# Handing over between stages by token tile, with a layer's modulation split between its attention and the feed-forward before it

## The chip, the cores and the metric

One core of a Trainium2 chip runs the whole kernel. The metric is the device time of one execution in microseconds (us). TensorE multiplies; VectorE, ScalarE and GpSimd work on data beside it; SyncE issues the large DMA transfers. In the profile PE is TensorE, PEld its weight loads, DVE VectorE, ACT ScalarE, POOL GpSimd and SP SyncE.

## The reference

A stack of four layers in fp32 with 256 tokens and a width of 1024, followed by one larger "latent" layer. Each of the four layers is an attention (layer 0 and 3 stick-breaking, 1 MoBA, 2 sliding window) and a gated feed-forward of width 2816; what goes into each is a normalised x, shifted and scaled by a modulation that is computed from a vector c.

```
for i in range(DEPTH):
    mod = silu(c) @ ada_w[i] + ada_b[i]                 # 1024 x 6144
    sh1, sc1, g1, sh2, sc2, g2 = split(mod, 6)
    h = rms_norm(x, norm_gain[i, 0]) * (1 + sc1) + sh1
    x = x + g1 * attention[i](h)                        # w_in, heads, w_out
    h = rms_norm(x, norm_gain[i, 1]) * (1 + sc2) + sh2
    x = x + g2 * ((silu(h @ w_gate[i]) * (h @ w_up[i])) @ w_down[i])
...
mod, mod_c = silu(c) @ w_ada + b_ada, silu(c_ctx) @ w_ada + b_ada   # latent layer: also for a context
...
```

## The kernel before

**Matrix multiplication.** A fp32 product is made of three TensorE passes (L1878 to L1880): each weight and each input is split into a high and a low part, and high x high, low x high and high x low are added up in PSUM. Weights come in units of 4 k-tiles (128 rows each) by 512 columns, 1 MB, into a ring of four buffers `raw`. ScalarE casts a unit into w_hi (L856), VectorE subtracts for w_lo (L1311), both double buffered, so the conversion of unit u + 2 waits until unit u is multiplied. SyncE issues the loads in the order of one list, `loads`, and a buffer is free again when VectorE is through with it.

**Modulation.** The 1024 x 6144 matrix of a layer comes through the same ring as 24 further units ("ada"). TensorE is not used for their product: VectorE multiplies each unit by 128 entries of c and adds it to an accumulator `acc` of 128 x 2048 (`modulation_units`, L1327, 2.35 us). Eight units make a block, three blocks a layer, and `acc` is double buffered over blocks; GpSimd sets a new one to zero and loads its bias (`start_sums`). Then TensorE sums over the 128 partitions (`modulation`): as rows (pieces r1 and r2, the gates g1 and g2; L1916) or as columns (pieces c0, c1 and c2, the shifts and scales; L1924), and ScalarE copies the result out (L867, L873). Block 0 holds c0, block 1 holds r1 and c1, block 2 holds c2 and r2. For the latent layer the first eight units are accumulated a second time, into `acc_c`, for the context.

**What sets the order.** Each engine's program is written out. The tables ADA_MIX, ADA_UP and ADA_DOWN say behind which step of an attention, of the up half or of the down half of a feed-forward an ada unit is loaded and accumulated; SUMS says where the sums stand. Steps of an attention are numbered n; two make a panel of 512 columns, and SLOTS places the steps of the softmax between them. Before, attention 0 takes 16 units (its own blocks 1 and 2), attentions 1 and 2 take 8 (the next layer's block 0), attention 3 none, and the feed-forwards 24, 16, 16 and 24.

**Between two stages.** The last product is in two halves of 512 columns. VectorE multiplies each by its gate and adds it to x_res (`residual`, L1385 and L1389; half 1 can start only at the end of the last unit). ScalarE takes the squares (L897), VectorE and ScalarE the root for both token tiles of 128 together, VectorE scales the rows to n_st (L1372), TensorE transposes them (L1896), ScalarE applies gain, scale and shift and casts, VectorE takes the low part (L1346), and the next unit can be multiplied. In a feed-forward the same path from gate x up (act_st, L1538) through a transpose (L2113) leads into the down half, whose 22 k-tiles per half of the columns are taken as five units of 4 and a last one of 2.

## Time and profile before

| | us |
|---|---|
| median of 3 runs | 2442.58 |
| lowest and highest run | 2432.83, 2444.14 |
| the profiled execution | 2443.3 |
| its span in the trace | 2441.5 |
| TensorE busy in it | 1987.2 (81%) |
| VectorE busy in it | 1402.3 (57%) |
| ScalarE busy in it | 956.5 (39%) |
| accumulations (L1327), 120 in all | 281.9 |

A busy TensorE is not one at its full clock: the granted clock (PEclk) is shown beside it as a share of 2.4 GHz. The stages that are spoken of below: attention 0 from 52 to 210 us, feed-forward 0 to 431, attention 1 to 644, feed-forward 1 to 866, attention 2 to 1038, feed-forward 2 to 1259, attention 3 to 1409, feed-forward 3 to 1648, then the latent layer to the end.

### The profile page before, as it was taken

To read this page: it belongs to the slowest core of one execution; us is meant where nothing else is said; L and a number is where in the kernel's file an instruction comes from. 1 tells how busy PE (TensorE), PEld (TensorE's weight loads), DVE (VectorE), ACT (ScalarE), POOL (GpSimd) and SP (SyncE) were. 2 spreads that over 40 slices of the span, in tenths; PEclk is the share of its full clock that TensorE was granted. 3 is DMA by queue.
4 is the path that set the end of the run, shared out by engine and by line. 5 is a ranking of instruction groups with operands and counts; after the bars stand their busy time and mean duration, and the time that the engine had idled before them with its cause. 6 is when DMAs were issued, how large, how long until landed. Compare 5 with 4: busy or idle time off the path is not lost.

```text
span 2441.5 us, 34110 instructions
## 1 busy us (share of the span) xinstructions
PE 1987.2 (81%) x14354; PEld 1608.0 (66%) x14354; DVE 1402.3 (57%) x1415; ACT 956.5 (39%) x1353; POOL 108.6 (4%) x135
## 2 busy tenths in 40 slices
PE   3887999765699984679989869996878878767998
PEld 2665787554578763468767657875666677765787
DVE  5774768655466564366644578574335663445554
ACT  3454443333444342344445534334223411224543
POOL 1000000101000011000000000001000112000000
PEclk9998999887799987689999979897879898978999
DMA  7653879542288662167753347683113100023553
GB/s 279 251 212 113 276 251 331 192 174 69 69 269 279 208 222 75 52 203 259 246 172 121 114 161 248 216 317 137 54 52 104 35 4 3 17 86 109 173 189 104
DMA packets 215117, 393.42 MB, mean 161 GB/s; under 512 B 11306, under 2 KB 130102, under 8 KB 199606
## 3 DMA queue, kind: packets, MB, share of 16 engines
q1 hardware_dynamic: 214453, 391.12, 46.9%
q8 instruction: 114, 1.87, 0.3%
q14 instruction: 38, 0.30, 0.0%
q0 software_dynamic: 512, 0.13, 0.0%
HBM read 390.17 MB, written 1.05 MB: 160 GB/s over the span
## 4 chain that ended last, share of the span: by engine, by line
PE 62%; DVE 18%; ACT 11%; issue 6%; DMA 2%; POOL 1%; DVEq 0%; SPq 0%; ACTq 0%
PE G L1878 15%; PE G L1879 15%; PE G L1880 15%; DVE w_lo L1311 6%; ACT w_hi L856 4%; DVE acc L1327 4%; PE A L1924 2%; PE A L2336 2%; PE A L1916 1%; PE A L1896 1%; ACT z_sb L966 1%; PE A L2113 1%; PE G L2350 1%; PE A L1984 1%; POOL e_sb L741 1%
## 5 line engine op out<-in xcount | busy, mean ns | idle before, releaser
L1311 DVE TENSOR_TENSOR w_lo<-raw,w_hi 128x2048 fp32r<-128x2048 f32 (+1 forms) x256 | 569.8, 2226 | 515.6 <-ACT w_hi L856 510.8
L856 ACT CAST w_hi<-raw 128x2048 fp32r<-128x2048 f32 (+1 forms) x256 | 475.2, 1856 | 688.9 <-PE G L1880 590.7
L1878 PE MATMUL G<-w_hi,h_hi 128*128 128x512 f32 (+1 forms) x1376 | 559.8, 407 | 90.0 <-DVE w_lo L1311 47.9
L1879 PE MATMUL G<-w_lo,h_hi 128*128 128x512 f32 (+1 forms) x1376 | 546.9, 397 | 0.0
L1880 PE MATMUL G<-w_hi,h_lo 128*128 128x512 f32 (+1 forms) x1376 | 545.4, 396 | 0.0
L1878 PEld LDWEIGHTS G<-w_hi,h_hi 128*128 128x128 f32 x1376 | 270.0, 196 | 152.9 <-issue 73.3
L1880 PEld LDWEIGHTS G<-w_hi,h_lo 128*128 128x128 f32 x1376 | 269.4, 196 | 57.1
L1879 PEld LDWEIGHTS G<-w_lo,h_hi 128*128 128x128 f32 x1376 | 270.1, 196 | 52.5 <-issue 0.5
L1878 PE MATMUL G<-w_hi,act_hi 128*128 128x512 f32 (+2 forms) x704 | 282.7, 401 | 20.2 <-DVE act_lo L1346 10.5
L1327 DVE SCALAR_TENSOR_TENSOR acc<-raw,c_col,acc 128x2048 f32<-128x2048 f32 x120 | 281.9, 2349 | 25.1 <-DVE w_lo L1311 12.6
L1879 PE MATMUL G<-w_lo,act_hi 128*128 128x512 f32 (+2 forms) x704 | 278.0, 395 | 0.0
L1880 PE MATMUL G<-w_hi,act_lo 128*128 128x512 f32 (+2 forms) x704 | 277.3, 394 | 0.0
L1878 PEld LDWEIGHTS G<-w_hi,act_hi 128*128 128x128 f32 x704 | 138.3, 196 | 52.2 <-DVE act_lo L1346 12.5
L1880 PEld LDWEIGHTS G<-w_hi,act_lo 128*128 128x128 f32 x704 | 138.0, 196 | 28.3
L1879 PEld LDWEIGHTS G<-w_lo,act_hi 128*128 128x128 f32 x704 | 138.6, 197 | 27.1 <-issue 0.5
L1346 DVE TENSOR_TENSOR act_lo<-full,act_hi 128x512 fp32r<-128x512 f32 (+1 forms) x86 | 57.7, 679 | 112.8 <-ACT act_hi L882 104.9
L1896 PE MATMUL A<-consts,n_st 128*128 128x128 f32 x176 | 34.9, 381 | 58.7 <-DVE n_st L1372 54.3
L753 POOL MEMSET acc<- 128x2048 f32 x15 | 27.1, 1808 | 1167.6 <-PE A L1924 996.6
L1924 PE MATMUL A<-consts,acc 128*128 128x1 f32 x320 | 45.6, 274 | 39.7 <-DVE acc L1327 35.3
L1896 PEld LDWEIGHTS A<-consts,n_st 128*128 128x128 f32 x176 | 31.4, 204 | 68.3 <-DVE n_st L1372 56.3
L1924 PEld LDWEIGHTS A<-consts,acc 128*128 128x128 f32 x320 | 46.1, 228 | 43.4 <-DVE acc L1327 36.3
L2043 PE MATMUL A<-consts,z_sb 128*128 128x128 f32 x32 | 8.9, 435 | 71.4 <-DVE z_sb L1491 71.4
(350 smaller groups left out, 2052.9 us busy)
## 6 DMA issues: line engine op xcount, KB each, us to landing
raw<-in_ada_w SPq DMA_DIRECT2D x96, 1024.0 KB, 5.1
raw<-in_ffn_w_gate SPq DMA_DIRECT2D x88, 512.0 KB, 3.9
raw<-in_ffn_w_up SPq DMA_DIRECT2D x88, 512.0 KB, 5.0
raw<-in_ffn_w_down SPq DMA_DIRECT2D x40, 1024.0 KB, 5.1
raw<-in_w_mlp SPq DMA_DIRECT2D x32, 1024.0 KB, 5.6
raw<-in_w_ada SPq DMA_DIRECT2D x24, 1024.0 KB, 5.0
raw<-in_w_in SPq DMA_DIRECT2D x18, 1024.0 KB, 5.0
raw<-in_sb_w_in SPq DMA_DIRECT2D x32, 512.0 KB, 4.7
```

The source lines that it names most:

```text
L741: ins = nc.gpsimd.tensor_tensor(dst[:, :, :, a:a + 32], src[:, :, :, b:b + 32], for_heads(rope_t[:, 1, t, tabs, a:a + 32], heads // (tabs. ...
L753: nc.gpsimd.memset(acc[:, b % 2], 0.0).then_inc(acc_zero, 1)
L856: nc.scalar.copy(w_hi[:, u % 2, 0:len(kts), 0:n], raw[:, slot].rearrange("p (k n) -> p k n", k=UNIT_K)[:, 0:len(kts), 0:n])\
L1311: nc.vector.tensor_tensor(w_lo[:, u % 2, 0:len(kts), 0:n], raw[:, slot].rearrange("p (k n) -> p k n", k=UNIT_K)[:, 0:len(kts), 0:n], w_hi[ ...
L1327: nc.vector.scalar_tensor_tensor(out=acc[:, b % 2], in0=raw[:, slot], scalar=c_col[:, c:c + 1], in1=acc[:, b % 2], op0=ALU.mult, op1=ALU.a ...
L1346: nc.vector.tensor_tensor(dst_lo, full[:, f % 2, 0:SEQ * dst_lo.shape[1]].rearrange("p (a n) -> p a n", n=SEQ), dst_hi.bitcast(F32), ALU.s ...
L1878: nc.tensor.matmul(banks[t][:, 0:n], x_hi[:, kt, ts], w_hi[:, u % 2, i, 0:n], start=st, stop=False)
L1879: nc.tensor.matmul(banks[t][:, 0:n], x_hi[:, kt, ts], w_lo[:, u % 2, i, 0:n], start=False, stop=False)
L1880: ins = nc.tensor.matmul(banks[t][:, 0:n], x_lo[:, kt, ts], w_hi[:, u % 2, i, 0:n], start=False, stop=en)
L1896: ins = nc.tensor.transpose(A[q][:, i * SEQ + t * P:i * SEQ + t * P + P], n_st[:, t, (2 * q + i) * P:(2 * q + i + 1) * P], ident)
L1924: ins = nc.tensor.matmul(banks[0][:, dst:dst + 1], x[:, c * P:c * P + P], ones[:, 0:1], start=True, stop=True)
L2336: ins = nc.tensor.matmul(A[c][half_of(1 - ch), cols_of(h)], LT[half_of(ch), c, cols_of(h)], X[half_of(ch), c, cols_of(h)], start=True, sto ...
```

## The change

It does two things.

**Hand-over by token tile.** After the last unit's products for token tile 0 TensorE gives a signal of its own (`tile_done`), and the last half's residual is taken tile by tile (`last_residual`, inside `norm`). Squares, root, scaling and the transposes of k-tiles 0 to 3 go tile by tile as well, and so do the splits behind them (128 x 4 x 128 instead of 128 x 512); k-tiles 4 to 7 go as before. One Newton step for the root takes two VectorE operations on one tile instead of four on both. A unit now waits for the split of its own tile (`ready_at`). The conversion of unit 1 stands between the tile splits and the others. The down half starts with the unit of 2 k-tiles (`down_kts`) instead of ending with it.

**Modulation.** Every attention takes 16 ada units, its own layer's blocks 1 and 2, spread evenly over its panels' steps; feed-forwards 0 to 2 take 8 (the next layer's block 0, three units of weights apart), feed-forward 3 takes 24 for the latent layer, spread from its second unit on. The sums r1 and c12 (c1 and c2 in one piece of 16 columns) stand behind the second step of the output projection of every attention, r2 behind up panel 1, c0 behind the down half's unit 8; in feed-forward 3 c0 stands behind up panel 7 and r1 behind down 2, and c12 and r2 behind the latent layer's first panel. The load of consts_2 goes out six loads later.

```diff
         for l in range(DEPTH):
-            first = KT if l in (1, 2) else 0
-            for i in range(first, ADA_U):
-                p = max(0, i - first - 2)
...
+            slots = 2 * len(qkv_panels(KINDS[l])) + 1
+            for i in range(2 * KT):
+                ADA_MIX[l].setdefault(i * slots // (2 * KT), []).append((l, KT + i))
+            n, first = (KT, 4) if l < DEPTH - 1 else (ADA_U, 2)
+            for i in range(n):
+                unit = first + i * (2 * FF // 256 + 6 - first) // n
+                if unit < 2 * (FF // 256):
+                    ADA_UP[l].setdefault(unit // 2, []).append((l + 1, i))
                 else:
...
+        SUMS = {(l, ("up", 1)): (l, "r2") for l in range(DEPTH)}
+        SUMS |= {(l, ("down", 8)): (l + 1, "c0") for l in range(DEPTH - 1)}
+        SUMS |= {(DEPTH - 1, ("up", 7)): (LAT, "c0"), (DEPTH - 1, ("down", 2)): (LAT, "r1")}
...
+        def down_kts(h):
+            return range(max(0, 4 * h - 2), 4 * h + 2)
...
@@ ScalarE, norm @@
-                rsqrt(NT)
-                for piece in sums or []:
-                    modulation(l, piece)
+                for t in range(NT):
+                    if x_end is not None and t == 0:
+                        k.tails += 1
+                        act.wait_ge(x_half, k.tails)
+                    elif x_end is not None:
+                        act.wait_ge(x_ready, x_end)
+                    square_of(t, 1, x).then_inc(ss_ready, 1)
+                    rsqrt(slice(t, t + 1))
...
@@ VectorE, norm @@
+                if last is not None:
+                    last_residual(0, *last)
+                mean_square(0)
+                if last is not None:
+                    last_residual(1, *last)
+                scale_rows(0)
+                mean_square(1)
+                scale_rows(1)
+                for t in range(NT):
+                    split(lo[:, 0:KT // 2, t * P:t * P + P], hi[:, 0:KT // 2, t * P:t * P + P])
                 between()
-                for q in range(KT // 2):
+                for q in range(KT // 4, KT // 2):
                     split(lo[:, 2 * q:2 * q + 2], hi[:, 2 * q:2 * q + 2])
...
@@ VectorE, mean_square and scale_rows @@
+                    nc.vector.scalar_tensor_tensor(out=rms_v[:, t:t + 1], in0=ssq[:, t, 1:2], scalar=1.0 / D, in1=ssum[:, t:t + 1],
+                    link(nc.vector.scalar_tensor_tensor(out=z, in0=y, scalar=y, in1=v, op0=ALU.mult, op1=ALU.mult))
+                    link(nc.vector.scalar_tensor_tensor(out=z, in0=z, scalar=-3.0, in1=y, op0=ALU.add, op1=ALU.mult))
+                    nc.vector.tensor_scalar(n_st[:, t], x[:, t], z, -0.5, ALU.mult, ALU.mult).then_inc(n_ready, 1)
...
@@ TensorE, unit @@
+                    if ready is not None:
+                        pe.wait_ge(split_lo, ready[t])
...
+                    if tiles and t == 0:
+                        ins.then_inc(tile_done, 1)
...
@@ TensorE, attention @@
-                        if l == 0 and n == 2 * len(panels) + 1:
-                            modulation(0, "r1")
-                            modulation(0, "c1")
+                        if n == 2 * len(panels) + 1:
+                            modulation(l, "r1")
+                            modulation(l, "c12")
...
-                if l == 0:
-                    modulation(0, "c2")
-                    modulation(0, "r2")
                 norm_transposes()
```

Where the order moves. VectorE, in the gap behind attention 1 (layer 1): n_st<-G,gates and x_res<-x_res,n_st are a residual, gsc the gain and scale, ssum to rms_y the root, h_lo the low parts for the feed-forward. Before:

```order
L1389 TENSOR_TENSOR x_res<-x_res,n_st 128x512 x2
L1385 TENSOR_TENSOR n_st<-G,gates 128x512 x2
L1389 TENSOR_TENSOR x_res<-x_res,n_st 128x512 x2
L1369 TENSOR_TENSOR ssum<-ssq 128x2
L1353 TENSOR_SCALAR rms_v<-ssum 128x2
L1355 TENSOR_TENSOR rms_t<-rms_y 128x2
L1356 TENSOR_TENSOR rms_t<-rms_t,rms_v 128x2
L1357 TENSOR_SCALAR rms_t<-rms_t 128x2
L1358 TENSOR_TENSOR rms_y<-rms_y,rms_t 128x2
L1372 TENSOR_SCALAR n_st<-x_res,rms_y 128x1024 x2
L1362 SCALAR_TENSOR_TENSOR gsc<-mod,cols 128x8
L1311 TENSOR_TENSOR w_lo<-raw,w_hi 128x2048
```

and now:

```order
L1377 SCALAR_TENSOR_TENSOR gsc<-mod,cols 128x8
L1385 TENSOR_SCALAR ssum<-ssq 128x2
L1426 TENSOR_TENSOR n_st<-G,gates 128x512
L1432 TENSOR_TENSOR x_res<-x_res,n_st 128x512
L1389 SCALAR_TENSOR_TENSOR rms_v<-ssq,ssum 128x1
L1426 TENSOR_TENSOR n_st<-G,gates 128x512
L1432 TENSOR_TENSOR x_res<-x_res,n_st 128x512
L1397 SCALAR_TENSOR_TENSOR rms_t<-rms_y,rms_v 128x1
L1398 SCALAR_TENSOR_TENSOR rms_t<-rms_t,rms_y 128x1
L1399 TENSOR_SCALAR n_st<-x_res,rms_t 128x1024
L1389 SCALAR_TENSOR_TENSOR rms_v<-ssq,ssum 128x1
L1397 SCALAR_TENSOR_TENSOR rms_t<-rms_y,rms_v 128x1
```

The residual of the second half is cut into tiles, and each tile's root and scaling follow one another; what is behind, the conversion w_lo, now stands after the first two splits.

VectorE, from the gap behind feed-forward 1 into attention 2 (ss_81 is the first operation of its query and key norm). Before:

```order
L1311 TENSOR_TENSOR w_lo<-raw,w_hi 128x4x256
L1346 TENSOR_TENSOR h_lo<-full,h_hi 128x512 x4
L1327 SCALAR_TENSOR_TENSOR acc<-raw,c_col,acc 128x2048
L1311 TENSOR_TENSOR w_lo<-raw,w_hi 128x2048
L1327 SCALAR_TENSOR_TENSOR acc<-raw,c_col,acc 128x2048
L1311 TENSOR_TENSOR w_lo<-raw,w_hi 128x2048
L1327 SCALAR_TENSOR_TENSOR acc<-raw,c_col,acc 128x2048
L1422 TENSOR_REDUCE ss_81<-e_sb 128x4
```

and now:

```order
L1361 TENSOR_TENSOR h_lo<-full,h_hi 128x4x128 x2
L1325 TENSOR_TENSOR w_lo<-raw,w_hi 128x4x256
L1361 TENSOR_TENSOR h_lo<-full,h_hi 128x512 x2
L1341 SCALAR_TENSOR_TENSOR acc<-raw,c_col,acc 128x2048 x3
L1325 TENSOR_TENSOR w_lo<-raw,w_hi 128x2048
L1341 SCALAR_TENSOR_TENSOR acc<-raw,c_col,acc 128x2048 x2
L1325 TENSOR_TENSOR w_lo<-raw,w_hi 128x2048
L1341 SCALAR_TENSOR_TENSOR acc<-raw,c_col,acc 128x2048 x2
L1478 TENSOR_REDUCE ss_81<-e_sb 128x4
```

Seven accumulations instead of three stand ahead of that norm.

TensorE, at the end of attention 1 (A<-aT,v_st are the last weighted values, G<-w_hi,act_hi begins another unit of the output projection). Before:

```order
L1984 MATMUL A<-aT,v_st 64x256
L1985 MATMUL A<-aT,v_st 64x128
L1984 MATMUL A<-aT,v_st 64x256
L1985 MATMUL A<-aT,v_st 64x128
L1878 MATMUL G<-w_hi,act_hi 128x512
```

and now:

```order
L2052 MATMUL A<-aT,v_st 64x256
L2053 MATMUL A<-aT,v_st 64x128
L2052 MATMUL A<-aT,v_st 64x256
L2053 MATMUL A<-aT,v_st 64x128
L1981 MATMUL A<-acc,consts 128x512 x2
L1992 MATMUL A<-consts,acc 128x1 x16
L1934 MATMUL G<-w_hi,act_hi 128x512
```

The row sums r1 and the 16 column sums c12 now stand between the two. The numbers behind an x here count instructions; the trace has two records for each of these fp32 ones.

## Rows read from the trace of the kernel before

**Rows 1.** The page, chain that ended last, by engine.

```profile
PE 62%; DVE 18%; ACT 11%; issue 6%; DMA 2%; POOL 1%; DVEq 0%; SPq 0%; ACTq 0%
```

**Rows 2.** Windows: stretch, length, busy (records) by engine, PEclk, DMA share, GB/s; then accumulations alone.

```profile
210.00:226.50 16.50, 7.36 (x35) 4.49 (x35) 10.23 (x19) 9.95 (x22) 2.29 (x2) 0.79 0.35 125
430.60:449.40 18.80, 9.21 (x36) 6.39 (x37) 12.94 (x18) 8.95 (x18) 5.19 (x8) 0.73 0.68 234
644.00:658.50 14.50, 3.65 (x16) 3.28 (x17) 10.20 (x19) 8.73 (x19) 0.00 (x0) 0.65 0.34 108
866.40:881.50 15.10, 9.14 (x38) 6.13 (x36) 7.70 (x16) 8.14 (x19) 5.12 (x9) 0.66 0.44 139
1275.00:1408.70 133.70, 123.81 (x600) 94.57 (x600) 65.61 (x63) 70.07 (x96) 2.30 (x2) 0.97 0.34 111
...
52.30:210.00 157.70, 37.62 (x16) 0.92 0.57 204
449.40:644.00 194.60, 18.81 (x8) 0.80 0.34 119
881.50:1038.50 157.00, 18.81 (x8) 0.75 0.30 108
```

**Rows 3.** Timeline, gap behind attention 1: start, us, engine, operation, [idle before, releaser].

```profile
643.07 1.29 DVE L1385 TENSOR_TENSOR n_st<-G,gates 128x512 f32<-128x512 f32 x2 [0.21 <-DVE w_lo L1311]
...
650.98 0.16 DVE L1355 TENSOR_TENSOR rms_t<-rms_y 128x2 f32<-128x2 f32 x1 [0.51 <-ACT rms_y L891]
...
651.77 1.42 DVE L1372 TENSOR_SCALAR n_st<-x_res,rms_y 128x1024 f32<-128x1024 f32 x2
...
648.75 0.62 ACT L897 ACTIVATE n_st<-x_res 128x512 f32<-128x512 f32 x1
...
653.29 3.65 PE L1896 MATMUL A<-consts,n_st 128*128 128x128 f32 x16 [9.32 <-DVE n_st L1372]
...
658.53 0.77 PE L1878 MATMUL G<-w_hi,h_hi 128*128 128x512 f32 x1 [1.59 <-issue]
```

**Rows 4.** Timeline, TensorE, from feed-forward 3 into the latent layer.

```profile
1651.76 3.57 PE L1924 MATMUL A<-consts,acc 128*128 128x1 f32 x16 [4.10 <-DVE acc L1327]
...
1680.26 0.36 PE L1878 MATMUL G<-w_hi,h_hi 128*128 128x256 f32 x1 [1.70 <-issue]
```

**Rows 5.** Timeline, VectorE, in attentions 1, 2 and 3.

```profile
559.52 0.20 DVE L1485 RECIPROCAL p_inv<-p_sum 128x8 f32<-128x8 f32 x1
...
926.84 2.14 DVE L1460 TENSOR_REDUCE n_max<-A 128x2 f32<-128x256 f32 x4 [0.65 <-PE A L2037]
...
1311.75 1.88 DVE L1410 TENSOR_TENSOR aT<-z_sb,A 128x512 f32<-128x512 f32 x3
```

**Rows 6.** Timeline, TensorE, at the end of attentions 0 and 3.

```profile
188.90 3.75 PE L1916 MATMUL A<-acc,consts 128*128 128x512 f32 x4 [0.77 <-ACT full L1008]
...
193.37 3.54 PE L1924 MATMUL A<-consts,acc 128*128 128x1 f32 x16 [0.72 <-issue]
...
1397.42 0.50 PE L1878 MATMUL G<-w_hi,act_hi 128*128 128x512 f32 x1 [2.05 <-DVE act_lo L1346]
```

**Rows 7.** Timeline, TensorE and VectorE, in feed-forwards 0 and 3.

```profile
247.77 1.12 PE L2113 MATMUL A<-consts,act_st 128*128 128x128 f32 x4 [4.63 <-DVE act_st L1538]
...
369.92 0.66 PE L2113 MATMUL A<-consts,act_st 128*128 128x128 f32 x4
...
1452.85 1.12 PE L2113 MATMUL A<-consts,act_st 128*128 128x128 f32 x4 [11.49 <-DVE act_st L1538]
...
1476.41 2.29 DVE L1311 TENSOR_TENSOR w_lo<-raw,w_hi 128x2048 fp32r<-128x2048 f32 x1 [0.25 <-DVE acc_c L1336]
...
1487.89 2.29 DVE L1311 TENSOR_TENSOR w_lo<-raw,w_hi 128x2048 fp32r<-128x2048 f32 x1 [0.27 <-ACT w_hi L856]
```

**Rows 8.** Windows as in the first group of them, two stretches of feed-forward 3.

```profile
1480.00:1500.00 20.00, 20.00 (x93) 16.43 (x92) 17.06 (x11) 9.15 (x11) 0.00 (x0) 1.00 0.82 275
1600.00:1620.00 20.00, 18.25 (x81) 14.83 (x80) 16.11 (x9) 5.46 (x4) 0.00 (x0) 1.00 0.97 350
```

## What I predicted before the changed kernel ran

> **What bounds the kernel now.** I read the page first: TensorE stands under 62% of the chain that ended last and VectorE under 18% [rows 1]. That average says little, so I cut the span at the ends of matrix multiplication into stages [rows 2]. In a feed-forward TensorE runs nearly without a pause and VectorE has room. In an attention it is the other way round: VectorE or the chain through it ends most waits. Between two stages TensorE multiplies nothing for 14.5 to 18.8 us; four of these nine gaps are in [rows 2]. I then read the timeline of VectorE, ScalarE and TensorE in one gap [rows 3], at the end of the attentions [rows 6] and around the feed-forward's first act_st [rows 7]. The change touches all three: it shortens the gaps, relieves the feed-forwards, and loads the attentions.
>
> **Gap after an attention (five of them).** Multiplication ended at 653.29 - 9.32 = 643.97; VectorE had its last conversion until 642.9, did residual 0, then residual 1, until 648.2; n_st was done at 651.77 + 1.42 = 653.2 and the next stage's first matmul started at 658.53, 14.56 us after the end. Now the order of work of the new code, with the same durations: 0.65 us for each of the two operations of a residual's tile, 0.8 for a square of 0.62 with its read-out, 0.7 from rms_v until rms_t may start (0.51 of it waiting for the root) [rows 3]. Residual 0 still ends at 645.7, since it waits for the conversion, not for the tile. VectorE then stands until ScalarE's two squares are done (647.1), does tile 0 of residual 1 (648.7), waits for its square (649.6), tile 1 (651.2), scales row tile 0 (652.4), waits for tile 1's root (653.0), scales tile 1 (654.2). The last n_st is 1.0 us later than before, not earlier: tile 0 being ready early buys nothing when VectorE is late. But only 12 transposes at 0.23 us follow instead of 16, and the first matmul needs tile 0 alone, whose split has long been done: it starts at 654.2 + 0.1 + 2.8 = 657.1. **Gain 1.4 us** each in four gaps. After attention 0 the r2 and c2 sums also leave the gap (16.5 against 13.2): 3.4. Sum -9.
>
> **Gap after a feed-forward.** Here VectorE is free 1.1 us before the end, because the last weight unit now has 4 k-tiles instead of 2. Same durations: residual tile 0 done at end + 0.7, tile 1 at 3.2, n_st at 4.4 and 6.2, first matmul at 9.1. Before: 15.1 to 18.8 us in the two that [rows 2] shows, since c2 and r2 stood there, once waiting for acc. But unit 1's conversion now comes after two splits, so TensorE is ready for unit 1 about 1 us before its data; and attention's first two accumulations sit in front of unit 2's. Net -9.5 (layer 0 to 1) and -6 (2 to 3); 1 to 2 is taken with its attention below. Into the last part, 1647.66 to 1680.26 = 32.6 us [rows 4] becomes 22.6 by the same count for both inputs, less 4.5 for c12 and r2, which now stand behind its first panel with ScalarE and GpSimd work behind them: -5.5. At the kernel's start -2. Sum -23.
>
> **Feed-forwards.** TensorE waited 4.63 us for act_st at 247.77 because three accumulations stood in front of it on VectorE; 11.49 us in layer 3 [rows 7]. In layers 0 to 2 eight accumulations are now spread three units apart, so the wait goes (4.6 to 4.9), with it some 1.7 us of slower matmuls behind it (the transposes at 247.77 take 1.12 us, those at 369.92 0.66), and one sums block of 1.8 moves to the attention. Against that the short weight unit is now the first: the transposes of act_st at 369.92 waited for nothing [rows 7], but their input is ready only some 5.5 us after the last up unit, and 2.8 us of matmuls no longer cover it: +2.7. Per layer -5.5, -7.7, -5.7. Layer 3 differs: the first eight modulation units there cost two operations of 2.35 us each with their waits, 4.86. One panel with one such unit takes VectorE 1487.89 - 1476.41 = 11.48 us, just TensorE's 11.49. Two per panel for four panels adds 4 x 4.86 = 19.4, less some 3 of slack; later panels with two single ones come to 11.7. So +16.4 + 3 + 2.7 against -11.5 - 1.7 - 3.6: +5. Sum -14.
>
> **Accumulations in the attentions.** Layer 0 has 16 before and after; layers 1 and 2 have 8 before and 16 after; layer 3 none and 16 [rows 2]. Each takes 37.62 / 16 = 2.35 us and 0.2 of waiting. I laid each new one into VectorE's timeline at its slot: where idle time stands in front of the next operation it is free, where the next operation starts at once it costs 2.56. In layer 3, slots 0, 3, 6 and 11 absorb theirs; slot 4 (two) stands right before aT at 1311.75 and costs 4.8 [rows 5], slots 7, 10 and 12 cost 2.3 to 2.6, slots 5, 8 and 9 0.4 to 2.9 together: +15.5. In layer 1, slots 8, 9 (before the reciprocal at 559.52, for whose product TensorE waits) and 12 cost 2.5 each, slot 11 1.1: +8.8. Layer 2 packs all 16 into its seven slots; VectorE is saturated there from 884 to 922, so n_max of 926.84 [rows 5], 60.4 us after the end of the feed-forward, comes at 77.5; one more at slot 6. With the gap's gain already taken off, +19.7. Layer 0: 16 as before but in other slots, +2. Cross-check: attention 0 and attention 3 are the same code, 157.7 us with 16 accumulations and 133.7 with none [rows 2]; 8.6 of the 24.0 is its sums, which leaves 0.96 per accumulation, against 0.97 by my count. Sum +46.
>
> **Sums in the attentions.** r1 and c12 now stand after the last weighted values in every layer. r1 took 3.75 and 16 records of c1 3.54 at the lower clock [rows 6]; c12 is 32: 3.75 + 0.7 + 7.1 + 0.1, less the wait of 2.05 for act_lo that they cover [rows 6] = 9.6, and up to 2 us more of slow matmuls behind them. Layers 1 to 3 +10, +9, +11.5, layer 0 +3 for the longer block: +33. At the full clock the records take half as long and the block would be +4.2 in each layer, about 17 less in all; this is the lower bound, and I take the upper one since the only such block in an attention, layer 0's, ran at the lower clock.
>
> **A rule weighed.** The mean granted clock is 0.65 of full speed in the gap at 644 and 0.79 in the one at 210 [rows 2]. If shorter gaps kept it up, the slow matmuls behind them would come back too, which is rival 4. The gaps speak against it so far: those of 14.5 and 15.1 us run at 0.65 and 0.66, no better than those of 16.5 and 18.8 (0.79 and 0.73, with sums in them) [rows 2]. The Trainium skill (TensorE: Matmul & The Clock Gate, HAM oscillation) has it that an idle TensorE falls to the lower clock and that shorter pauses keep it up; the trace agrees with the fall and not yet with the second half, and by that rule the sum would end at rival 4's 2462.
>
> **Sum.** -9 - 23 - 14 + 46 + 33 = +33. The profiled execution has a span of 2441.5 us and 1.8 around it; 2441.5 + 33 + 1.8 = 2476, and the median of the runs lies 0.7 below the profiled one: **2476 us**.
>
> **Rivals.**
> (1) *The accumulations hide.* VectorE is busy 65.6 of 133.7 us in attention 3 [rows 2]; if its idle time takes the new 32 in wherever they stand, about 50 us of the +46 and the gain of the gap before layer 2 fall away: 2476 - 50 = 2426, faster. It decides at the 32 accumulations costing (50 - 33) / 32 = 0.5 us each. Against it: the cross-check above, and that the operation that the chain needs next starts within 0.2 us of the conversion before it at 559.52 and 1311.75 [rows 5].
> (2) *Sums at full clock, gaps as counted, half of layer 2's load absorbed.* 17 + 9 less: 2450, within the noise.
> (3) *Weights starve.* 16 units of 1 MB in seven slots of layer 2 and two per panel in layer 3 take places in a ring of four; at the rate of the stretch at 1480 (275 GB/s) [rows 8] a panel of 4.2 MB takes 15.2 us instead of 11.7 (six panels: +20) and layer 2 some 5 more: 2501. It decides where a panel's rate stays under 4.2 / 11.7 = 359 GB/s for long. Against it: between 1600 and 1620 the queues moved 350 GB/s [rows 8], and the demand at 1480 was no greater than what came.
> (4) *The clock stays up through the shorter gaps.* The first matmul behind the gap takes 0.77 us [rows 3] and 0.50 where the clock was up [rows 6]; seven or eight slower ones make some 1.6 us, nine times 14: 2462. Against it stands the comparison of the gaps above.
>
> **Chances.** The forecast (2458 to 2495) 0.55, (1) 0.15, (2) 0.13, (3) 0.10, (4) 0.07. Half a per cent, about what a measurement of this kernel tells from no change, is 12 us: faster 0.15, same 0.15, slower 0.70. The range takes in (2), (4) and most of (3), not (1): 2435 to 2500.
>
> **What would show it.** In the profile after: 13 us from the last multiplication of an attention to the next first matmul, 9 after a feed-forward; the 4.6 us wait before the first act_st gone; attention 3 at about 160 us with 16 accumulations, close to attention 0; n_max of layer 2 at 77 us behind the feed-forward's end; r1 and c12 over 11 us in attentions 1 to 3; feed-forward 3 at some 230 us. I am wrong if attention 3 stays under 145 us or the block of sums takes under 7.

## The result and the profile after

| | before | after |
|---|---|---|
| median of the runs, us | 2437.89 (4 runs) | 2475.33 (4 runs) |
| lowest and highest, us | 2432.83, 2444.14 | 2472.84, 2479.85 |
| the profiled execution, us | 2443.3 | 2479.85 |
| its span, us | 2441.5 | 2478.1 |

The ratio after to before is 1.0154, with a 95% interval of 1.012 to 1.0188: the changed kernel is 1.5% slower. I had predicted 2476, from a median before of 2442.58 over three runs; with the fourth run that median is 2437.89, so the measured change is +37.4 us where I had +33.

The page, its chain that ended last by engine, of the changed kernel:

```profile
PE 58%; DVE 23%; ACT 12%; issue 5%; POOL 1%; DMA 1%; DVEq 0%; SPq 0%; ACTq 0%
```

Against [rows 1], 4 points of the chain have gone from TensorE and 5 have come to VectorE. The windows say where. Here are four gaps, from the last multiplication of a stage to the first of the next, and attention 3 (stretch, length, busy and records by engine, PEclk, DMA share, GB/s), then the accumulations alone in attentions 0 to 3:

```profile
209.70:222.20 12.50, 3.63 (x17) 3.15 (x17) 7.74 (x18) 6.57 (x20) 0.00 (x0) 0.69 0.28 85
423.70:432.20 8.50, 3.63 (x18) 3.19 (x17) 5.10 (x13) 5.27 (x16) 0.00 (x0) 0.64 0.38 125
647.00:659.40 12.40, 3.56 (x16) 3.14 (x16) 7.67 (x18) 6.53 (x20) 0.00 (x0) 0.67 0.27 84
860.50:867.50 7.00, 3.69 (x18) 3.21 (x17) 4.31 (x10) 4.41 (x14) 0.00 (x0) 0.67 0.18 76
1280.70:1438.20 157.50, 135.91 (x638) 103.00 (x636) 105.85 (x81) 75.18 (x104) 4.58 (x4) 0.94 0.59 207
...
49.90:209.70 159.80, 37.62 (x16) 0.93 0.58 204
432.20:647.00 214.80, 37.62 (x16) 0.78 0.43 152
867.50:1058.60 191.10, 37.61 (x16) 0.71 0.38 138
1280.70:1438.20 157.50, 37.61 (x16) 0.94 0.59 207
```

These answer to [rows 2]. All gaps are shorter (16.5, 18.8, 14.5 and 15.1 have become 12.5, 8.5, 12.4 and 7.0); attention 3 has grown from 133.7 to 157.5, attention 1 from 194.6 to 214.8, attention 2 from 157.0 to 191.1.

The whole difference, cut at the ends of multiplication in both traces and in the main experiments. "Gap" is the stretch behind the stage named; all in us. The experiments' short names are explained below.

| stage | before | after | ffn24 | ffn24_sums | acc_small | inter |
|---|---|---|---|---|---|---|
| start | 52.3 | 49.9 | 49.3 | 49.3 | 49.3 | 49.2 |
| attention 0 | 157.7 | 159.8 | 157.5 | 160.1 | 160.3 | 157.6 |
| gap | 16.6 | 12.5 | 12.5 | 12.5 | 12.5 | 12.5 |
| feed-forward 0 | 204.0 | 201.5 | 211.0 | 217.4 | 201.5 | 201.3 |
| gap | 18.9 | 8.5 | 8.5 | 8.5 | 8.5 | 8.7 |
| attention 1 | 194.6 | 214.8 | 195.2 | 187.5 | 194.5 | 194.6 |
| gap | 14.6 | 12.5 | 12.5 | 12.5 | 12.5 | 12.5 |
| feed-forward 1 | 207.9 | 201.1 | 210.1 | 218.6 | 201.3 | 205.2 |
| gap | 15.0 | 6.9 | 6.9 | 6.9 | 6.9 | 6.5 |
| attention 2 | 157.0 | 191.1 | 156.4 | 149.3 | 178.7 | 153.9 |
| gap | 14.6 | 12.5 | 12.5 | 12.5 | 12.5 | 12.5 |
| feed-forward 2 | 205.7 | 201.2 | 210.1 | 220.3 | 201.3 | 203.4 |
| gap | 16.2 | 8.5 | 8.5 | 8.5 | 8.5 | 8.4 |
| attention 3 | 133.7 | 157.5 | 140.0 | 133.9 | 143.0 | 141.6 |
| gap | 14.6 | 12.5 | 12.5 | 12.5 | 12.5 | 12.5 |
| feed-forward 3 | 224.5 | 240.1 | 237.1 | 232.4 | 232.4 | 223.3 |
| gap | 32.6 | 19.9 | 19.9 | 19.9 | 19.9 | 20.5 |
| latent layer, with its two gaps | 761.2 | 767.4 | 767.8 | 758.0 | 764.5 | 763.0 |
| span | 2441.5 | 2478.1 | 2427.9 | 2420.4 | 2420.5 | 2387.0 |

So the gaps (the one inside the latent layer among them) and the start give back 54 us, and the attentions take 80. The table also shows how far a single trace can be trusted. The latent layer behind its gap differs by up to 10 us between kernels that have the same code there, and attention 0 by up to 2.8. Feed-forwards 0 to 2 of the changed kernel and of acc_small, again the same code, agree within 0.2.

**The gap behind attention 1**, timeline of the changed kernel (start, us, engine, operation, idle before and what ended it):

```profile
647.40 1.29 DVE L1445 TENSOR_TENSOR x_res<-x_res,n_st 128x512 f32<-128x512 f32 x2
...
650.10 0.17 DVE L1385 TENSOR_SCALAR ssum<-ssq 128x2 f32<-128x2 f32 x1 [1.32 <-ACT n_st L902]
650.30 0.69 DVE L1426 TENSOR_TENSOR n_st<-G,gates 128x512 f32<-128x512 f32 x1
...
655.25 1.09 PE L1952 MATMUL A<-consts,n_st 128*128 128x128 f32 x4 [8.27 <-DVE n_st L1399]
...
656.12 0.75 DVE L1399 TENSOR_SCALAR n_st<-x_res,rms_t 128x1024 f32<-128x1024 f32 x1
...
659.45 0.76 PE L1934 MATMUL G<-w_hi,h_hi 128*128 128x512 f32 x1
```

Multiplication ended at 646.98. Residual 0 ends at 648.7 and VectorE stands for 1.32 us until the squares of the first half are there, as in my sketch; the last n_st is done at 656.87, 9.9 us behind the end (I had 10.2), and the first product comes 12.47 behind it (I had 13.1). Compare [rows 3]: 14.56.

### The profile page after: what moved, and what is told of

Its sections match the earlier page's. It is cut to its first block, busy times and chain, and to the rows that moved or that the text cites. A ratio compares the mean times of both kernels' runs of the same rounds, so it can differ in the third digit from the quotient of the medians.

```text
span 2478.1 us, 34169 instructions
## 1 busy us (share of the span) xinstructions
PE 2014.1 (81%) x14354; PEld 1628.5 (66%) x14354; DVE 1406.8 (57%) x1426; ACT 972.5 (39%) x1414; POOL 106.9 (4%) x135
## 4 chain that ended last, share of the span: by engine, by line
PE 58%; DVE 23%; ACT 12%; issue 5%; POOL 1%; DMA 1%; DVEq 0%; SPq 0%; ACTq 0%
PE G L1934 14%; PE G L1935 14%; PE G L1936 14%; DVE w_lo L1325 8%; DVE acc L1341 6%; ACT w_hi L862 4%; PE A L1992 2%; PE A L2398 1%; ACT full L925 1%; ACT z_sb L991 1%; POOL e_sb L747 1%; PE A L2177 1%; PE G L2412 1%; PE A L1981 1%; PE A L2410 1%
## 5 line engine op out<-in xcount | busy, mean ns | idle before, releaser
L1934 PE MATMUL G<-w_hi,h_hi 128*128 128x512 f32 (+1 forms) x1376 | 569.1, 414 | 93.2 <-DVE w_lo L1325 41.1
L1935 PE MATMUL G<-w_lo,h_hi 128*128 128x512 f32 (+1 forms) x1376 | 553.0, 402 | 0.0
L1936 PE MATMUL G<-w_hi,h_lo 128*128 128x512 f32 (+1 forms) x1376 | 551.2, 401 | 0.0
L1934 PEld LDWEIGHTS G<-w_hi,h_hi 128*128 128x128 f32 x1376 | 275.7, 200 | 160.4 <-issue 78.8
L1935 PEld LDWEIGHTS G<-w_lo,h_hi 128*128 128x128 f32 x1376 | 275.6, 200 | 53.4 <-issue 1.0
L1952 PE MATMUL A<-consts,n_st 128*128 128x128 f32 x88 | 23.3, 418 | 76.9 <-DVE n_st L1399 76.9
L1952 PEld LDWEIGHTS A<-consts,n_st 128*128 128x128 f32 x88 | 15.2, 210 | 85.1 <-issue 73.9
```

The costliest lines, as they stand in the source:

```text
L1934: nc.tensor.matmul(banks[t][:, 0:n], x_hi[:, kt, ts], w_hi[:, u % 2, i, 0:n], start=st, stop=False)
L1935: nc.tensor.matmul(banks[t][:, 0:n], x_hi[:, kt, ts], w_lo[:, u % 2, i, 0:n], start=False, stop=False)
L1936: ins = nc.tensor.matmul(banks[t][:, 0:n], x_lo[:, kt, ts], w_hi[:, u % 2, i, 0:n], start=False, stop=en)
L1952: ins = nc.tensor.transpose(A[t][:, c * P:c * P + P], n_st[:, t, c * P:c * P + P], ident)
```

## The experiments

Ten more kernels ran. They take the changed kernel apart along the three questions that the prediction left: what an accumulation costs in an attention, what a sum costs, and what the early signal and the short first unit bring.

### One or two blocks moved back into the feed-forward (ffn16, ffn24)

```diff
-            for i in range(2 * KT):
+            for i in range(2 * KT if l == 0 else 0):
                 ADA_MIX[l].setdefault(i * slots // (2 * KT), []).append((l, KT + i))
-            n, first = (KT, 4) if l < DEPTH - 1 else (ADA_U, 2)
+            n, first = ADA_U, 2
...
-        SUMS |= {(l, ("down", 8)): (l + 1, "c0") for l in range(DEPTH - 1)}
-        SUMS |= {(DEPTH - 1, ("up", 7)): (LAT, "c0"), (DEPTH - 1, ("down", 2)): (LAT, "r1")}
+        SUMS |= {(l, ("up", 7)): (l + 1, "c0") for l in range(DEPTH)}
+        SUMS |= {(DEPTH - 1, ("down", 2)): (LAT, "r1")}
```

This is ffn24; ffn16 moves block 1 alone and leaves c0 where it is.

> The changed kernel with one of the three blocks (8 accumulations, and their loads) taken out of attentions 1 to 3 and put back into the feed-forward before, spread over its units; r1 and c12 stay at the end of the attention. If each accumulation in an attention costs VectorE time on the chain (my theory), attention 1 falls by about 11 us, attention 2 by 20 to 25, attention 3 by about 9, and the three feed-forwards rise by 1 to 3 each: 2435 to 2445. If the accumulations hide and the loss is in the sums and the clock (rival 1), it stays within 10 us of the changed kernel's 2475.

> The changed kernel with no accumulation in attentions 1 to 3 and 24 in each feed-forward (c0 summed behind up panel 7); r1 and c12 still at the end of the attention. My theory: attention 3 back at 133.7 + 6 for its sums = about 140, attentions 1 and 2 at 180 to 190 and 150 to 155; each feed-forward waits 3 to 6 us more for act_st or a conversion: 2415 to 2430. If the feed-forwards have no room (the rival on VectorE as bound there): each takes 10 to 15 more and the sum stays at 2445 or above.

ffn16: 2445.4 us, 1.0024 of before (1.0004 to 1.0043). ffn24: 2429.5 us, 0.9967 (0.9947 to 0.9987). The first is 0.4 us outside what my theory expected, the second within it. Attention 1 went 214.8, 202.5, 195.2 with 16, 8 and 0 accumulations; attention 2 191.1, 167.6, 156.4; attention 3 157.5, 147.5, 140.0. Rival 1, that the accumulations hide, is out: 16 of them are worth 19.6, 34.7 and 17.5 us in the three attentions, 1.1 to 2.2 us each, where it needed under 0.5. The feed-forwards rose from 201 to 207.6 and to 210 to 211; I had them too cheap in both.

### The accumulations without their arithmetic, then without their bytes (acc_small, nobytes)

```diff
-                    nc.vector.scalar_tensor_tensor(out=acc[:, b % 2], in0=raw[:, slot], ...
+                    w_ = 16 if 1 <= l < LAT and n >= KT else 2 * D
+                    nc.vector.scalar_tensor_tensor(out=acc[:, b % 2, 0:w_], in0=raw[:, slot, 0:w_], ...
```

and, for nobytes, 512 instead of 2048 columns in the load of the same units of layer 2. Both leave out most of the modulation of layers 1 to 3.

> The changed kernel with the accumulations of blocks 1 and 2 for layers 1 to 3 cut to their first 16 of 2048 columns (the rest of the modulation is left out); their loads, places in the ring and waits stay. If VectorE's time is what they cost, attentions 1 to 3 fall to 185, 150 and 142 us and the whole to about 2415. If the loads and the ring of four buffers are what costs (rival 3), the attentions stay at 215, 191 and 157 and the whole at 2470 or above.

> The changed kernel with the accumulations of blocks 1 and 2 of layers 1 to 3 cut to 16 columns, as in the run acc_small, and in layer 2 their loads cut to a quarter of the bytes as well (most of the modulation is left out); the number of loads, their places in the ring and all waits stay. In acc_small attention 2 took 178.7 us, against 156.4 with no such units at all. If the bytes are what costs (DMA moved 373 to 392 GB/s there and ScalarE's cast waited 19.4 us for weights of w_in), attention 2 falls to 157 to 162 us. If it is the places in the ring and the order of waits, it stays at 175 or above. Attentions 1 and 3 stay at 194 and 143.

acc_small took 2419.8 us (0.991 of before, 0.9884 to 0.9936), nobytes 2421.1 in its one execution. Attentions 1 to 3 of acc_small took 194.5, 178.7 and 143.0 us, where I had expected 185, 150 and 142. Accumulations alone in attentions 1 and 2 of it:

```profile
432.10:626.60 194.50, 3.75 (x16) 0.82 0.47 168
847.30:1026.00 178.70, 3.75 (x16) 0.72 0.40 147
```

33.9 us of VectorE work less in each (37.62 to 3.75), and attention 1 is 20.3 us shorter, attention 3 14.5, attention 2 only 12.4. In attentions 1 and 3 that is all or nearly all there was: without any such units (ffn24) they stand at 195.2 and 140.0. In attention 2 it is a third. There ScalarE's casts wait for weights in both kernels, and neither in the kernel before nor in ffn24. What ScalarE waited for in attention 2 (total, times, longest, us), the changed kernel, then acc_small, then nobytes:

```profile
ACT w_hi L862 <- DMA raw<-in_swa_w_in: 19.2, 3, 8.4
```

```profile
ACT w_hi L862 <- DMA raw<-in_swa_w_in: 19.4, 4, 9.7
```

```profile
ACT w_hi L863 <- DMA raw<-in_swa_w_in: 10.8, 3, 3.8
```

And the DMA rate in the first half of that attention, windows of acc_small and of nobytes (columns as above):

```profile
860.00:880.00 20.00, 16.05 (x59) 12.65 (x60) 9.19 (x21) 5.50 (x7) 1.31 (x4) 0.84 0.97 374
880.00:900.00 20.00, 11.44 (x43) 8.73 (x41) 9.35 (x16) 5.20 (x5) 3.73 (x4) 0.83 0.93 363
```

```profile
860.00:880.00 20.00, 17.01 (x65) 13.86 (x66) 12.25 (x23) 6.69 (x12) 1.33 (x4) 0.83 0.55 182
880.00:900.00 20.00, 12.79 (x53) 9.82 (x53) 11.96 (x18) 5.67 (x6) 3.73 (x4) 0.82 0.52 184
```

In acc_small the queues are busy for 0.93 to 0.97 of the time at 363 to 374 GB/s, and the weights that TensorE needs next stand in the same queue behind ada units. The DMA issues from 867 to 935 us of the changed kernel (count, KB each, median us to landing):

```profile
raw<-in_ada_w SPq DMA_DIRECT2D x13, 1024.0 KB, 5.8
raw<-in_swa_w_in SPq DMA_DIRECT2D x4, 1024.0 KB, 5.2
raw<-in_swa_w_out SPq DMA_DIRECT2D x2, 1024.0 KB, 5.3
```

With a quarter of the bytes attention 2 took 168.6 us, 10.1 less than acc_small; I had expected 157 to 162 if the bytes were what costs and 175 or above if they were not, and it lies between. The remaining 12.2 us against ffn24 are the 16 places in the ring, the handling of each unit, and the quarter of the bytes that stayed; which of them, no run separates. So for layer 2 rival 3 (weights starve) was right beside the main theory: of 34.7 us, 12.4 are VectorE's arithmetic, 10.1 bytes, 12.2 this rest. The split holds for this order of taking away; what the arithmetic costs with the bytes gone, no run shows. Each part is a difference of two single traces, and attention 2 took 191.1 and 186.5 us in two kernels with the same code in it (the changed one and late_tile, below).

### The sums in the feed-forward (ffn24_sums, fewcols)

```diff
+        SUMS |= {(l, ("down", 2)): (l + 1, "r1") for l in range(DEPTH)}
+        SUMS |= {(l, ("down", 8)): (l + 1, "c12") for l in range(DEPTH - 1)}
...
-                        if n == 2 * len(panels) + 1:
+                        if l == 0 and n == 2 * len(panels) + 1:
                             modulation(l, "r1")
                             modulation(l, "c12")
```

> As the one without accumulations in attentions 1 to 3, and r1 and c12 of the next layer summed in the feed-forward (behind down units 2 and 8), where TensorE's granted clock is full. The block measured 9.1, 9.1 and 6.4 us in attentions 1 to 3 of the changed kernel; at the full clock the records are half as long and in a feed-forward nothing else waits for them: 4.2 us each there. Expected 10 to 14 us less than with the sums in the attentions: 2402 to 2418. If a sum costs the same wherever it stands: no difference.

2424.4 us, 0.9949 of before (0.993 to 0.9968), 5 less than ffn24 where 10 to 14 were expected. The block left the attentions and took 7.7, 7.1 and 6.1 us with it, against 9 to 11.5 in my sum. (The run fewcols below has the same attentions and gives 8.6, 9.8 and 5.3, so each price is good to some 3 us.) The timeline of TensorE in attentions 1 and 3 of the changed kernel shows why it differs by layer:

```profile
625.24 3.04 PE L1981 MATMUL A<-acc,consts 128*128 128x512 f32 x4
629.05 5.35 PE L1992 MATMUL A<-consts,acc 128*128 128x1 f32 x32 [0.77 <-ACT gates L873]
...
1419.16 1.98 PE L1981 MATMUL A<-acc,consts 128*128 128x512 f32 x4
1421.91 3.70 PE L1992 MATMUL A<-consts,acc 128*128 128x1 f32 x32 [0.77 <-ACT gates L873]
```

I had taken the 7.1 us of the lower clock for the 32 records of the columns. In attention 3 they ran almost wholly at the full one (3.70).

But feed-forwards 0 to 2 rose by 6.4, 8.5 and 10.2 us, where the sums' records there take 5.35 and nothing waits for them. The products of feed-forwards 1 and 2 took 3.4 and 4.7 us longer (189.3 against 184.6 in the latter) with the same idle time. Feed-forward 2 of ffn24_sums, the 32 records and a window ahead of them and one behind them (TensorE alone: stretch, length, busy, PEclk, DMA share, GB/s):

```profile
1233.58 3.63 PE L1993 MATMUL A<-consts,acc 128*128 128x1 f32 x32
...
1213.00:1233.40 20.40, 18.65 (x83) 1.00 0.85 307
1237.40:1255.20 17.80, 17.80 (x72) 0.90 0.37 118
```

TensorE has no idle time behind the sums and still its granted clock is 0.90 there, while it was 1.00 ahead of them with 1.75 us idle. The suspicion was that the single-column products themselves pull it down. So fewcols cuts c12 there from 16 columns to 4 and leaves out the rest of the shift and scale:

> The kernel with all accumulations and all sums in the feed-forwards (the run ffn24_sums), with the 16 column sums of c12 of layers 1 to 3 cut to 4 (the rest of the shift and scale is left out). Their records took 3.63 us at full clock, and the multiplications of that feed-forward were 4 to 5 us slower than without them, the granted clock 0.91 behind them. If the column sums pull the clock down, feed-forwards 0 to 2 fall by more than the 2.7 us of the records, by 5 to 7 us each (from 217.4, 218.6 and 220.3). If the slower products have another cause, they fall by 2.7 us.

2416.4 us in its one execution; feed-forwards 0 to 2 at 213.1, 212.7 and 212.8, that is 4.3, 5.9 and 7.5 us less, and products in feed-forward 2 at 185.2 us. The window behind its 8 records, and the same products at the end of that feed-forward in ffn24, which has no sums there:

```profile
1215.40:1231.90 16.50, 16.45 (x73) 1.00 0.58 185
```

```profile
1225.80:1242.30 16.50, 16.47 (x73) 1.00 0.58 192
```

With 24 records fewer the clock stays at 1.00, as with none. From the block's first record to the end of the stage it is 21.7 us in ffn24_sums and 17.4 in fewcols, in each of the three feed-forwards: of these 4.3 us, 2.7 are the records that went and 1.6 the products behind them. The rest of the fall, 0.0, 1.5 and 3.2 us, lies ahead of the block, where the two kernels have the same code, so it is not the work of the block.

The changed kernel has such a block of its own, the 32 records of c0 behind the down half's unit 8. Windows behind it in feed-forwards 0 to 2 (TensorE alone):

```profile
405.70:423.60 17.90, 17.90 (x72) 0.91 0.35 119
842.60:860.40 17.80, 17.80 (x72) 0.91 0.46 148
1253.10:1272.20 19.10, 19.10 (x72) 0.85 0.33 111
```

It does not always happen. In the up halves of the kernel before, 32 such records at 701.05 were followed by 20 us at 1.00:

```profile
704.80:724.80 20.00, 20.00 (x92) 1.00 0.75 246
```

So moving the sums out of the attentions brought next to nothing in those stages (20.9 us less there, 25.1 more in the feed-forwards): of the 25.1, some 16 are the records, 5 the slower products behind c12, and 4 lie ahead of it. In the two traces the difference comes from elsewhere, feed-forward 3 and the latent layer, where the code is the same. The 5 us between the medians are hardly more than the scatter of the runs (2425.1 to 2438.9 and 2420.2 to 2435.7).

### The early signal and the short first unit (late_tile, before_short_first)

```diff
@@ late_tile, VectorE, last_residual @@
-                    dve.wait_ge(tile_done, k.tails)
+                    dve.wait_ge(gemm_done, u_end)
@@ before_short_first, in the kernel before, the loads and TensorE @@
-range(4 * h, min(4 * h + 4, FFT))
+range(max(0, 4 * h - 2), 4 * h + 2)
```

> The changed kernel, but VectorE starts the residual of token tile 0 only when the whole last unit is multiplied (the early signal isn't used; everything else of the hand-over by tile stays). My step says that in the gap behind an attention the early signal buys nothing, since VectorE comes late from its last conversion: 12.47 us stays 12.5 there; behind a feed-forward VectorE is free early and the gap grows by 1.3 to 3 us (from 8.5 and 6.9). The rival says that the early signal is what shortened all gaps: both kinds grow by 2 us or more.

> The kernel before with one edit of the change alone: the down half of a feed-forward starts with the unit of 2 k-tiles. My sum says that the transposes of the last act_st then wait about 2.7 us that 2.8 us of matmuls covered before, and that the gap behind the feed-forward gets about 1 us shorter since VectorE has its last full conversion behind it earlier: feed-forwards 0 to 2 at +2.7, gaps 2, 4, 6 at -1, in all 4 to 8 us slower than the kernel before. The rival says that the last act_st comes in time and the edit only gains: feed-forwards the same, 3 to 5 us faster.

late_tile took 2475.7 us in one execution, what the changed kernel takes: its gaps are 6.7 us longer in all, but attention 2 is 4.6 and the latent layer's first part 6.1 us shorter, with the same code. So only the gaps say something. Those behind the attentions stay at 12.48; the ones behind the feed-forwards go from 8.5, 6.9, 8.5 and 19.9 to 9.3, 9.3, 9.3 and 22.7. First transposes behind feed-forward 1, the changed kernel and late_tile:

```profile
863.25 1.09 PE L1952 MATMUL A<-consts,n_st 128*128 128x128 f32 x4 [2.71 <-DVE n_st L1399]
```

```profile
865.05 1.09 PE L1952 MATMUL A<-consts,n_st 128*128 128x128 f32 x4 [5.05 <-DVE n_st L1399]
```

and behind attention 1, late_tile; the idle time is the same 8.27 as above:

```profile
654.50 1.09 PE L1952 MATMUL A<-consts,n_st 128*128 128x128 f32 x4 [8.27 <-DVE n_st L1399]
```

So the signal for tile 0 (I had expected 1.3 to 3 us behind a feed-forward) is worth 0.8 to 2.8 us behind a feed-forward and nothing behind an attention, as the prediction's first step said. Of the 51.5 us that the gaps gained, the other 45 come from the rest: the sums gone, 12 transposes instead of 16, fewer small operations, a unit waiting only for its own tile. No run separates these.

before_short_first: 1.0014 of before (0.9989 to 1.0039), no difference that can be told. Its feed-forwards 0 to 2 are 3.0, 3.4 and 5.7 us longer (the waits for act_st are 7.3, 7.8 and 7.6 us in place of 4.6, 4.9 and 4.9, as predicted), its gaps 2.7, 0.0 and 1.3 shorter. The mechanism is there; the sum of 4 to 8 that I expected for the whole is not resolved. Its attention 0 took 152.4 us against 157.7, with the same code: again the scatter of one trace.

### A version that beats both (inter, inter_long)

ffn24 left one thing: TensorE waited 10.8 us a feed-forward for act_st, since two accumulations in a row stood in front of it on VectorE. inter spreads the 24 so that at most one stands behind each unit, and puts one between the two units of a panel (the edit against ffn24):

```diff
-            n, first = ADA_U, 2
+            n = ADA_U
...
+                unit = 1 + i * 3 // 2 if i < 14 else 2 * (FF // 256) + i - 14
...
-                loads += [next(ahead) for _ in range(2 if p else 1)]
-                loads += [("ada", *a) for a in ADA_UP[l].get(p, [])]
+                for h in range(2):
+                    if p or h:
+                        loads.append(next(ahead))
+                    loads += [("ada", *a) for a in ADA_UP[l].get(2 * p + h, [])]
...
                         act_mul(p - 1)
+                        modulation_units()
                         convert()
```

c0 is then summed behind up panel 9, and in feed-forward 3 r1 behind down 4. inter_long has the units of the down half in the order of the kernel before as well.

> Hand-over by tile as changed; no accumulations in attentions 1 to 3; in every feed-forward 24, of which 14 in the up half (every 1.5 units, at most one behind each unit, so that between the two units of a panel one stands behind act_st instead of two in a row in front of it) and 10 in the down half. r1 and c12 at the end of the attention. In the run ffn24 TensorE waited 10.95 us per feed-forward for act_st, against 2.64 with 8 accumulations. If the packing of two in a row makes these waits, they fall to 3 to 6 us and feed-forwards 0 to 2 from 210 to 203 to 206, feed-forward 3 from 237 to 228 to 233: 2404 to 2418 in all. If VectorE is simply full there (24 units cost what they cost), it stays at 2425 to 2430.

> As the run inter, with the down half's units in the order of the kernel before (2 k-tiles last). From before_short_first: feed-forwards get 3 us shorter each (the wait for the last act_st covered again), and the gap behind each grows by what VectorE's later last conversion costs, 1 to 3 us. If the two cancel, within 5 us of inter. If the cover is worth more, 5 to 10 us faster.

inter: 2390.4 us, 0.9803 of before (0.9786 to 0.9819). inter_long: 2388.8 us, 0.980 (0.9784 to 0.9817). The two can't be told apart: feed-forwards 2.4 to 5.8 us shorter, the gaps behind them 2.3 to 3.4 longer. inter came 14 us below my range (2404 to 2418): feed-forwards 0 to 2 took 203 on average, the lower end of what I expected, but feed-forward 3 took 223.3 us where I had 228 to 233. inter_long came within 5 us of inter, as expected if the two effects cancel. What ended the idle time in front of the transposes of act_st in feed-forward 2 (total, times), ffn24 and then inter:

```profile
  DVE act_st L1594: 10.8, 8
```

```profile
  DVE act_st L1596: 2.6, 1
```

Accumulations in feed-forward 0 of inter (busy, PEclk, DMA share, GB/s):

```profile
221.70:419.50 197.80, 56.40 (x24) 0.99 0.84 290
```

24 accumulations, 56.4 us of VectorE's time, and the feed-forward takes the 201 us that it takes with 8; feed-forwards 1 and 2 take 4.1 and 2.2 more than with 8. Most of what ffn24 lost there was not VectorE's load but where the operations stood: of the 27.4 us by which its feed-forwards 0 to 2 were longer than the changed kernel's, 21.3 came back. The even spacing and the new place between two units came in one edit, and no run separates them.

## Why the prediction was right, point by point

The figure came out within a microsecond; its terms did not all. Measured by the profiled spans (+36.6 against +33):

| term | predicted | measured |
|---|---|---|
| gaps behind attentions | -9 | -12.5 |
| gaps behind feed-forwards without the one ahead of attention 2, start, and the latent layer's first part | -23 | -26.7 |
| feed-forwards 0 to 2 | -19 | -13.8 |
| feed-forward 3 | +5 | +15.6 |
| accumulations and sums in the attentions, less the gap ahead of attention 2 | +79 | +72.2 |
| the rest of the latent layer | 0 | +1.7 |

**Gaps.** Right in mechanism. Each gap behind an attention gained 2.1 instead of 1.4 (4.1 instead of 3.4 for the first), the others came to 8.5 us, and 6.9 behind feed-forward 1, in place of my 9.1.

**Accumulations.** Adding up stages and taking the block of sums at its measured price, the accumulations cost attention 1 12.5 us (I had 8.8), attention 2 27.0, or 18.9 with the gap's gain of 8.1 taken off (I had 19.7), and attention 3 17.7 (I had 15.5). Attention 0, with accumulations and sums together, cost 2.1 where I had 5. The step that laid each accumulation into VectorE's timeline holds for attentions 1 and 3, where taking the arithmetic away gives it all back. n_max of attention 2 came 75.4 us behind the feed-forward's end (I had 77.5):

```profile
935.91 1.95 DVE L1516 TENSOR_REDUCE n_max<-A 128x2 f32<-128x256 f32 x4
```

That number was right for a reason that was a third of the truth. I wrote that VectorE is saturated in the first part of attention 2, and it is; but with its arithmetic taken away n_max still came 65.9 us behind the feed-forward's end, with a quarter of the bytes 59.0, and without the units (ffn24) 47.7. I had rival 3 decide at a rate under 359 GB/s, and had looked at feed-forward 3. In attention 2 of acc_small the queues ran at 363 to 374 and the weights were still late. My reading is that what counts there is not a rate per panel but 13 ada units in the queue among 6 of weights.

**Sums.** A step that failed in size: +30.5 for layers 1 to 3, 20.9 measured. I took the lower clock for the whole block from the one case in [rows 6]; in attention 3 most of it ran at full clock. I had expected the block to take over 11 us in all three and named one under 7 as a sign that I am wrong. It took 9.2 us in attention 1, and in attention 3, from 1419.16 to the end of the columns, 6.5: there the sign came true.

**Feed-forwards.** Feed-forward 0 gave 2.5 instead of 5.5: the wait for the first act_st went as I said, but the 1.7 us that I had for slow products behind it did not come back (products took 185.2 us against 184.0). The lower clock now stood in other places, behind the wait for the last act_st and behind c0's columns, shown above; my sum had no price for the latter.

Feed-forward 3 is the largest miss, 10.6 us. What ended the idle time in front of its transposes of act_st, before and after:

```profile
  DVE act_st L1538: 15.1, 3
```

```profile
  DVE act_st L1594: 23.0, 7
```

and the whole stage, before and after (columns as in the windows above):

```profile
1423.20:1647.70 224.50, 207.65 (x920) 170.13 (x920) 163.47 (x103) 86.19 (x93) 2.29 (x2) 0.93 0.72 246
```

```profile
1450.70:1690.80 240.10, 215.26 (x910) 174.46 (x908) 170.71 (x112) 92.12 (x102) 4.58 (x4) 0.92 0.69 237
```

The idle time grew by 8.0 us. My sum had 10.6 for it (16.4 + 3 + 2.7 - 11.5), so laying the doubled units into VectorE's timeline was not the error. The error is in TensorE's own work, where I had 5.3 less (1.7 of slow products and 3.6 of sums) and 7.6 more came. The sums took 14.7 us before and 14.9 after, since r2 of layer 3 came into the stage as c1 of the latent layer left it. And I had priced only the slow products behind the one long wait that went, not those behind the seven waits of 2.1 to 5.0 us that came in its place. Besides its first few us, the stage before has the clock at 0.50 in two stretches (from the wait of 11.49 us on, and at the columns of the latent layer); the stage after has six, five of them in or just behind waits for act_st. Windows of TensorE in two of these, behind the waits of 4.96 and 2.20 us:

```profile
1487.00:1491.00 4.00, 4.00 (x12) 0.50 1.05 341
1604.00:1607.00 3.00, 3.00 (x9) 0.50 1.00 337
```

It is not a property of the schedule alone: with the same code the stage took 232.4 us in acc_small and ffn24_sums, 237.1 in ffn24, and 240 in the changed kernel, late_tile and fewcols, with idle times within 1.7 us of each other.

**The rivals.** (1) is out by ffn16 and ffn24. (2), cheap sums, was nearer than I had it (20.9 us in layers 1 to 3, between the 12.6 of the full clock and my 30.5), but not with half of layer 2's load absorbed. (3) was true in one place that I had not priced well and false in the other. (4) is out: the granted clock is 0.64 to 0.69 in the gaps of 8.5 and 12.5 us, and 0.67 in the one of 7.0, and the first product behind a gap takes what it took in [rows 3]: 0.76 us at 659.45, shown above, and behind the gap of 8.5:

```profile
432.18 0.77 PE L1934 MATMUL G<-w_hi,h_hi 128*128 128x512 f32 x1
```

There was also less to win than its 14 us. [rows 3] shows one gap that ended at the lower clock, but behind seven of the ten gaps of the kernel before the first product was a fast one, even behind another attention with the same gap of 14.6 us:

```profile
1053.02 0.47 PE L1878 MATMUL G<-w_hi,h_hi 128*128 128x512 f32 x1 [1.71 <-issue]
```

After the change it is slow behind all ten. Over the 15 us behind each gap the granted clock was 0.95 in the mean before and is 0.92 now: the shorter gaps gave no clock back. The Trainium skill (TensorE: Matmul & The Clock Gate, HAM oscillation) asks for short pauses if the clock is to stay up. The longest pauses inside the gaps are still 8.27 us behind an attention and 2.71 behind feed-forward 1, and the traces agree that the clock falls in gaps with such pauses; whether shorter ones keep it up, no run here shows.

The agreement of the total is thus partly luck: sums 9.6 us too dear and feed-forward 3 10.6 us too cheap cancel, and what is left of the difference, +37.4 against +33, went into a median before that lay 4.7 us lower than the one I had started from.

## What to carry to other kernels

Work that fills an engine's idle time is free only where it stands in front of an operation that nobody waits for. 16 accumulations cost 1.1 to 2.2 us each in an attention, 0.6 in a feed-forward when two stand in a row ahead of what TensorE waits for, and 0 to 0.3 when at most one stands behind each unit. So before moving such work to another stage, first move it by one place within its own.

When a stage takes its weights through the same queue as the work that is moved there, lay out both engines' timelines: take away the arithmetic, then the bytes, since the one can hide the other.

## What the runs showed of the hardware

Blocks of single-column products were followed by a lower clock with TensorE busy throughout. Behind 32 of them (3.63 us) at the end of a feed-forward the next 17.8 to 19.1 us had a granted clock of 0.85 to 0.91, in all three feed-forwards of the changed kernel, and 0.90 in feed-forward 2 of ffn24_sums; behind 8 and behind none it was 1.00. It is no rule without exception: behind 32 in the up half of feed-forward 1 of the kernel before it was 1.00.

One core's queues moved 363 and 374 GB/s over 20 us each (acc_small, 860 to 900 us), more than the 350 of [rows 8].

With the same code, feed-forward 3 took from 232.4 to 240.1 us from one kernel to another. A difference under some 8 us in that stage of one trace proves nothing. In feed-forwards 0 to 2, where the clock falls less often, the changed kernel and acc_small agree within 0.2, and nobytes is 2 us off in one of the three.
